# A gated delta rule's solve moved earlier, key norms moved into one block, and a convolution tap moved from VectorE to ScalarE and GpSimd

## The reference

```python
u = rmsnorm(h, norm_mix); proj = u @ w_in                       # 1024 tokens, 1024 -> 2824
aq, ak, av, dq, dk, dv, dz, db, da = split(proj)
qkv = silu(causal_conv(concat(dq, dk, dv), conv_w))             # four taps for each channel
qc, kc = l2norm(q) * 128 ** -0.5, l2norm(k)                     # 4 heads of 128
beta = sigmoid(b); g = -exp(a_log) * softplus(a + dt_bias)
# in chunks of tokens, g a running sum inside a chunk:
L = strict_lower((k * beta) @ k.T * exp(g_i - g_j))
T = (I + L)^-1                                                  # the solve
u = T @ (v * beta);  w = T @ (k * beta * exp(g))
# scan over the chunks: v_new = u - w @ S; o = (q*exp(g)) @ S + a_qk @ v_new; S = S*d + k_d.T @ v_new
```

## Time and profile before

| | us |
|---|---|
| median of three runs | 2007.3 (2006.78 to 2010.78) |
| the profiled execution's own time | 2006.78 |
| its span, first to last instruction | 2005.0 |
| TensorE busy | 1918.5, 96% of the span |
| VectorE busy | 1202.4, 60% |
| ScalarE busy | 794.9, 40% |
| GpSimd busy | 559.6, 28% |
| mean granted TensorE clock | 0.982 of full |

### The profile page before, as it was taken

One profiled execution on the slowest core, in us unless ns is written; L12 is line 12 of the kernel. 1 busy time (PEld: TensorE's weight loads), 2 busy tenths in 40 slices (PEclk: granted clock), 3 DMA queues, 4 the chain that ended last, 5 costly groups with the idle time before them and its releaser, 6 DMA issues.

```text
span 2005.0 us, 24453 instructions
## 1 busy us (share of the span) xinstructions
PE 1918.5 (96%) x9573; PEld 1583.0 (79%) x9573; DVE 1202.4 (60%) x1802; ACT 794.9 (40%) x1409; POOL 559.6 (28%) x561
## 2 busy tenths in 40 slices
PE   8999899989998999999999999999999999799999
PEld 6778788877776888887788887778988897577687
DVE  4577444454489766658768788446435347566641
ACT  5766122254454333333233335434111136455521
POOL 0041014640074656550000023461523124111100
PEclk9999999998999999999999999999999999899999
DMA  5143422211132454449755520113111314311133
GB/s 154 42 146 107 124 78 87 93 53 42 43 116 93 149 173 132 157 157 393 283 178 207 188 64 28 40 51 127 44 31 32 116 43 143 115 32 33 42 91 98
DMA packets 226187, 216.77 MB, mean 108 GB/s; under 512 B 37320, under 2 KB 166600, under 8 KB 225560
## 3 DMA queue, kind: packets, MB, share of 16 engines
q1 hardware_dynamic: 226072, 215.21, 33.3%
HBM read 154.31 MB, written 60.87 MB: 107 GB/s over the span
## 4 chain that ended last, share of the span: by engine, by line
PE 76%; DVE 11%; ACT 5%; POOL 4%; issue 2%; DMA 2%; SPq 0%; DVEq 0%; POOLq 0%; ACTq 0%
PE ps L337 10%; PE ps L338 10%; PE ps L339 10%; PE ps L1769 4%; PE ps L1770 4%; PE ps L1771 4%; PE ps L2148 4%; PE ps L2150 4%; PE ps L2149 4%; PE ps L350 4%; PE ps L3467 3%; PE ps L574 2%; PE ps L1283 1%; PE ps L3368 1%; DVE fm L978 1%
## 5 line engine op out<-in xcount | busy, mean ns | idle before, releaser
L337 PE MATMUL ps<-xh,whi 128*128 128x512 f32 (+2 forms) x1216 | 484.9, 399 | 10.4 <-DVE wlo L323 5.1
L338 PE MATMUL ps<-xl,whi 128*128 128x512 f32 (+2 forms) x1216 | 464.7, 382 | 0.0
L339 PE MATMUL ps<-xh,wlo 128*128 128x512 f32 (+2 forms) x1216 | 463.9, 382 | 0.0
L337 PEld LDWEIGHTS ps<-xh,whi 128*128 128x128 f32 x1216 | 232.0, 191 | 54.2 <-DVE wlo L323 6.1
L339 PEld LDWEIGHTS ps<-xh,wlo 128*128 128x128 f32 x1216 | 231.7, 191 | 41.6
L338 PEld LDWEIGHTS ps<-xl,whi 128*128 128x128 f32 x1216 | 232.2, 191 | 36.6 <-issue 2.6
L1769 PE MATMUL ps<-oph,wsh 128*128 128x512 f32 x448 | 177.5, 396 | 13.1 <-DVE stu L1881 6.6
L2148 PE MATMUL ps<-dnh_b,dnh_a 128*128 128x512 f32 x448 | 175.8, 392 | 7.5 <-DVE dn_b L2174 7.5
L1770 PE MATMUL ps<-opl,wsh 128*128 128x512 f32 x448 | 176.3, 394 | 0.0
L1771 PE MATMUL ps<-oph,wsl 128*128 128x512 f32 x448 | 176.1, 393 | 0.0
L2150 PE MATMUL ps<-dnh_b,dn_a 128*128 128x512 f32 x448 | 175.5, 392 | 0.0
(11 more groups left out here) (495 smaller groups left out, 3469.1 us busy)
## 6 DMA issues: line engine op xcount, KB each, us to landing
dnr_b<-ff_d SPq DMA_DIRECT2D x28, 1024.0 KB, 7.8
dnr_a<-w_down SPq DMA_DIRECT2D x28, 1024.0 KB, 5.5
wraw<-w_in SPq DMA_DIRECT2D x47, 512.0 KB, 3.9
ff_d<-st SPq DMA_DIRECT2D x64, 256.0 KB, 5.1
ff_d<-stt SPq DMA_DIRECT2D x48, 256.0 KB, 5.1
upx<-w_up SPq DMA_DIRECT2D x16, 512.0 KB, 4.3
upy<-w_up SPq DMA_DIRECT2D x16, 512.0 KB, 5.6
xt<-x SPq DMA_DIRECT2D x8, 512.0 KB, 7.7
```

The lines of the kernel that those rows point to most:

```text
L337: pe.matmul(out, h, xh[:, xk, c0:c1_], start=(n == 0), stop=False)
L338: pe.matmul(out, h, xl[:, xk, c0:c1_], start=False, stop=False)
L339: mm = pe.matmul(out, l, xh[:, xk, c0:c1_], start=False, stop=(n == nk - 1))
```

## The change

It has four parts.

1. GpSimd: the key norms of all eight chunks run in one block, behind the turn of k3, with the Dg of chunks 0 and 1 after the first of them. Before, the two Dg ran in panel 4, three norms in the block, and five after the steps of panel 6. Chunk 0's kT and g move from slot 5 to slot 4 of panel 6.
2. The solve's first rows move to panel 10 (rows 1 to 3), ahead of the taps of v1. No rows stand behind the taps any more.
3. For the v panels tap 3 is a product on ScalarE into a new buffer `fm3`, added by GpSimd to what VectorE has after tap 2; silu waits for that add. The solve's temporary `gtmp` makes room for `fm3`.
4. SyncE: the loads of the queries come behind the stores of the inverse (their buffer overlaps the new `gtmp`), and Tw is loaded ahead of Rw for chunk 0.

```diff
-    Gb, gtmp = M("Gb", 32, [32, 32]), M("gtmp", 94, [256])
+    Gb, gtmp = M("Gb", 32, [32, 32]), M("gtmp", 40, [256])
+    fm3 = M("fm3", 92, [T])
-    solve_rows = {(11, 0): range(1, 7), (11, 1): range(7, 10), (11, 2): range(10, 12), (12, 0): range(12, 16), (12, 1): range(16, 19),
-                  (12, 2): range(19, 22), (13, 0): range(22, 32)}
+    solve_rows = {(10, 1): range(1, 4), (11, 0): range(4, 8), (11, 1): range(8, 13), (12, 0): range(13, 18), (12, 1): range(18, 24),
+                  (13, 0): range(24, 32)}
-                out[4 * hf + (n == 0)] += [("kT", n), ("g", n)]
+                out[4 * hf] += [("kT", n), ("g", n)]
+    def last_tap(kind):
+        return 2 if kind == "v" else 3
...
# silu (ScalarE)
+                if kind == "v":
+                    w.wait_ge(*pool_in.at("conv", "v", j))
+                else:
+                    w.wait_ge(*dve_in.at(*(("ev", kind, j, 512) if kind == "dz" else ("conv", kind, j, 3))))
# behind tap 0 (ScalarE)
+                if kind == "v":
+                    if j > 0:
+                        w.wait_ge(*pool_in.at("conv", "v", j - 1))
+                    act.activation(fm3[:], fmc[:, 3:T + 3], ACT.Copy, scale=conv_taps(kind, j)[:, 3:4]).then_inc(*act_in.up("conv3", j))
# VectorE
-                for tap in range(1, 4):
+                for tap in range(1, last_tap(kind) + 1):
-            for row in solve_rows.get((i, 2), ()):
-                solve_dve(dve, w, row)
# GpSimd, behind the turn of k3 (before: key_norm(range(3)), and range(3, NB) and the Dg elsewhere)
+                for b in range(NB):
+                    pool.tensor_tensor(tkh[:, b, :, :], tkh[:, b, :, :], bc(sm["rk"][:, 4 * b:4 * b + 4].unsqueeze(2), [128, 4, 128]), ALU.mult
+                                       ).then_inc(*pool_in.up("normed", kind, b))
+                    if b == 0:
+                        for n in range(2):
+                            delta_pool(pool, w, "diag", n)
+            if kind == "v":
+                w.wait_ge(*act_in.at("conv3", j))
+                w.wait_ge(*dve_in.at("conv", kind, j, 2))
+                pool.tensor_tensor(fms1[i % 2][:], fms1[i % 2][:], fm3[:], ALU.add).then_inc(*pool_in.up("conv", "v", j))
# SyncE
-                queries(0)
-                queries(1)
                 w.wait_ge(*dve_in.at("row", 30))
                 sp.dma_start(inv_d, Gb[:]).then_inc(*st_inverse.up())
                 w.wait_ge(*dve_in.at("inverse turned"))
                 sp.dma_start(invT_d, GT[:]).then_inc(*st_turned.up())
+                queries(0)
+                queries(1)
+                inverse_straight(0)
                 inverse_turned(0)
-                inverse_straight(0)
```

More of the change, by code:

```diff
@@ L882, in silu @@
             if kind in ("k", "q", "v", "dz"):
-                w.wait_ge(*dve_in.at(*(("ev", kind, j, 512) if kind == "dz" else ("conv", kind, j, 3))))
+                if kind == "v":
+                    w.wait_ge(*pool_in.at("conv", "v", j))
+                else:
+                    w.wait_ge(*dve_in.at(*(("ev", kind, j, 512) if kind == "dz" else ("conv", kind, j, 3))))
                 act.activation(fms1[i % 2][:], fms1[i % 2][:], ACT.Silu).then_inc(*act_in.up("silu", kind, j))
@@ L955, in project_dve @@
                 if conv and i > 1 and c0 == 0:
-                    w.wait_ge(*dve_in.at("conv", *in_panels[i - 1], 3))
+                    w.wait_ge(*dve_in.at("conv", *in_panels[i - 1], last_tap(in_panels[i - 1][0])))
+                    if in_panels[i - 1][0] == "v":
+                        w.wait_ge(*act_in.at("conv3", in_panels[i - 1][1]))
                 if kind == "av":
@@ L1027, in query_rope_pool @@
         w.wait_ge(*act_in.at("turned", "aq", 3, 1))
-        w.wait_ge(*dve_in.at("conv", "v", 3, 3))
+        w.wait_ge(*pool_in.at("conv", "v", 3))
+        w.wait_ge(*dve_in.at("conv", "v", 3, 2))
         w.wait_ge(*ld_c1.at())
@@ L1038, in project_pool @@
         pool.memset(fmc[:, 0:3], 0.0).then_inc(*pool_in.up("pad"))
-        def key_norm(blocks):
-            for b in blocks:
-                pool.tensor_tensor(tkh[:, b, :, :], tkh[:, b, :, :], bc(sm["rk"][:, 4 * b:4 * b + 4].unsqueeze(2), [128, 4, 128]), ALU.mult
-                                   ).then_inc(*pool_in.up("normed", "k", b))
         def turned(kind, j):
@@ L1048, in turned @@
                 w.wait_ge(*dve_in.at("norm", kind))
-                key_norm(range(3))
+                for b in range(NB):
[4 more added lines that the diff above has]
+                            delta_pool(pool, w, "diag", n)
             if kind == "dz":
@@ L1061, in project_pool @@
                 turned(*in_panels[i - 1])
-            if i == 4:
-                for n in range(2):
-                    delta_pool(pool, w, "diag", n)
-            if i == PREP0:
-                key_norm(range(3, NB))
+            if kind == "v":
+                w.wait_ge(*act_in.at("conv3", j))
+                w.wait_ge(*dve_in.at("conv", kind, j, 2))
+                pool.tensor_tensor(fms1[i % 2][:], fms1[i % 2][:], fm3[:], ALU.add).then_inc(*pool_in.up("conv", "v", j))
             if i == 1:
```

## The result

The changed kernel took 2026.4 us (median of 4 runs, 2019.5 to 2027.7) where the kernel before took 2007.5 on the same chip (4 runs, 2006.8 to 2010.8). The ratio over all of these runs is 1.0081, 95% interval 1.0059 to 1.0102, or 16.3 us more (11.8 to 20.5); the two medians alone are 18.9 apart. Slower, as forecast, but by more than the range allowed. The three intervals meet between 11.8 and 13.3 us. The profiled execution took 2025.3 us, its span is 2023.5.

The account below looks back on a forecast made before the run. TensorE carries 76% of the last chain; its large stop is 6.1 us idle at UR 0. Sum: 2006.8 + 5.2 (GT later) + 4.5 (additions) + 0.6 (queue) + 0 (clock) = 2017.1 us, range 2010 to 2022.

Parts of the forecast that it names:

- the late chain through g 1: Projection stage: norms ahead of mt 0 end it at 113.1, 7.2 us later; g 1 starts 6.4 later, at 115.8.
- the new wait of VectorE ahead of row 1: Panel 10: VectorE arrives at 176.7 and waits 6.4 us for Gb, until 183.1.
- the collision: V panels: GpSimd's adds hold up two-input VectorE steps for 0.8 of each add, 4.5 us together.
- a slack of 1.3 us: Solve's start: Gb lands at 178.4, row 1 started at 179.70; shifted 4.7 to 183.1, row 1 is 3.4 later.
- the queue: DMA queue from GT to UR 0: Rw issued behind Tw, 0.6 us more; query loads taken at 0.
- shift of the last Gb loads: From panel 8 on: VectorE 4.6 and TensorE 5.0 us late, so Gb's loads move by 4.7.
- work from row 1 to GT: VectorE's solve: one split (1.2) and one evacuation (0.6) come in, 1.8 us more.
- the clock's 2.1 us: TensorE at g 1: a wait of 5 us lowers the clock, charged 2.1 us.
- a gain at UR 0: TensorE at UR 0: last wait only 2.5 us, so the 2.1 us lost to the lower clock fall away.
- a load of this kind lands about 1.3 us after its last issue: Landing of Gb's last blocks, by Rw's example: issued from 175.69 on, 1.47 us, so landed at 178.4.
- a rival of 5.7: Additions in the v panels: the whole add blocks VectorE, losing 5.7 us, kernel at 2018; no separate chance given.
- The rival of more: Clock also drops at the turns of v1 and v3, or norms take 1.29: 2019 to 2022; chance 0.08.

Follow-up runs that it names:

- The three intervals: Changed kernel against the kernel before, measured three times: 16.3 us more (11.8 to 20.5), 11.5 (8.9 to 13.9) and 9.9 (6.6 to 13.3).
- the two later measurements: The changed kernel, unchanged, measured again against the kernel before: ratios 1.0057 and 1.0049, 11.5 and 9.9 us more.
- the whole: The changed kernel with all four parts against the kernel before: ratios 1.0081, 1.0057 and 1.0049 in three measurements.
- the two without taps: Changed kernel with the four taps back on VectorE, measured twice against the kernel before: 12.7 and 10.7 us more.
- the norms alone: The kernel before with only part 1 (key norms in one block, slot 4 for chunk 0): ratio 1.0035, 7.0 us more.
- the two later profiles of before: The kernel before, unchanged, profiled a second and a third time: 2011.8 and 2013.5 us.
- rows alone: The kernel before with only part 2 (solve rows from panel 10, none behind the taps): ratio 1.0033, 6.6 us more.
- later joins: The kernel before with chunk 0's joins two or three slots later on TensorE: 2.6 and 4.0 us less.

## Why the prediction came out as it did

Forecast: GT and UR 0 9.7 and 10.3 us later, 2017.1 us. UR 0 was 14.4 us later (net, mean of three), and the time 10 to 16 us. The direction was right, and so were the late chain through g 1, the new wait of VectorE ahead of row 1 and the collision. The size of the sum was short by 4.1 us at UR 0: 1.4 for key products that it didn't list, 1.1 for a shift taken too small, 1.0 for a slack of 1.3 us that wasn't there, 0.4 for the queue and 0.2 for the additions. The step that failed as a reading is the slack; the largest term is the one put at nothing. Term by term, from the means of three profiles after and two of before:

| term | predicted | measured |
|---|---|---|
| shift of the last Gb loads | 4.7 | 5.8 |
| less the slack of row 1 against their landing | 1.3 | 0.3 |
| row 1 | 3.4 | 5.5 |
| work from row 1 to GT | 1.8 | 1.8 |
| steps beside the additions | 4.5 | 4.7 |
| steps beside the key products | not listed | 1.4 |
| GT to UR 0 | 0.6 | 1.0 |
| UR 0 | 10.3 | 14.4 |

This doesn't account for the first time alone. By the forecast's own start, 2006.8, and 14.4 us the kernel would have taken 2021.2, inside the range. The median of 2026.4 lies 5.2 above that, and the profile puts most of it ahead of all that the change touches: the sum started from 2006.8, the own time of the odd execution whose turn of k1 came 3.9 us earlier than the changed kernel's, and whose clock stayed at its full level behind the turn of k0. On the other chips the kernel before took about 2013. That the two later measurements (11.5 and 9.9) stand near the forecast's 10.3 is luck too: UR 0 was 14.4 and 14.2 late in their profiles, and stretches that the change doesn't touch gave some of it back (5.0 us in the attention stage in the one, 2.0 between UR 0 and the attention in the other).

- *Right: mt 0, ms 0 and g 1.* Ahead of mt 0 stand eleven instructions at 1.0 us and one split. Mt 0 ended at 116.81 (112.9 less the 3.9 of the turn of k1), predicted 113.1. G 1 came at 115.6 on the same count, predicted 115.8. Its idle time, though, was 2.5 us and not 5, since TensorE had lost time ahead of it: 0.9 at kT 0, 1.3 at g 0, and the clock at the lower level behind them (g 0 took 2.07 us, and the granted clock was 0.66 from 105 to 110).
- *Mis-sized: the shift carried from there, 4.7.* The taps of q1 gave back 1.1 us and not 1.8 (4.58 in place of 5.68; one of the three still took 1.94 beside a Dg). And where the clock also fell at g 1 (a stretch at the lower level around 120 in all three profiles of the whole, in one of the two without taps, not with the norms alone), TensorE and not VectorE carried the shift. Counted from the turn of k1, g 2 starts at 55.0 us without this drop and at 56.5 to 56.6 with it, behind the same stop of 2.4 to 2.5 us, and g 7 at 95.9 and at 97.4 to 97.6 (kernel before: 48.8 and 91.4), so the drop is worth 1.5 us. The last Gb loads came 5.8 us late in the whole, and in the two kernels without taps 4.6 without the drop at g 1 and 6.0 with it; the norms alone had 4.0. The prediction charged the clock's 2.1 us once and set them against a gain at UR 0. Such a gain there was in the third profile only (UR 0 took 1.08 us, behind 1.8 idle), and there the clock had fallen at the turn of v3 instead (0.55 from 225 to 230 us). In the other two, UR 0 waited 4.5 us and took 1.9, as before.
- *Failed: "a load of this kind lands about 1.3 us after its last issue", so "at 178.4".* For Rw that is so, after the change too: 236.97 + 1.86 = 238.83, and UR 0 at 240.19, 1.4 us later. It doesn't carry over to Gb, though both are loads of 16 KB each. The blocks of Gb released row 1 2.8 us behind their last issue in the changed kernel and 3.1 us in the two later profiles of before, in which row 1 waits for them (2.6 to 3.3 in all 14 profiles in which it waits). So there was no slack of 1.3 us to take up part of the shift, only the 0.3 between 3.1 and 2.8. Why Gb takes longer than Rw stays open. In the profile that I had, row 1 started right behind the evacuation, at 179.70; it bounded the landing from above, at 179.7 (2.5 us behind the last issue), and I put it 1.3 us below that with no row for it.
- *Right: VectorE waits ahead of row 1*, 8.1 us and not 6.4, and the 1.8 us of work that moves behind it. The saved taps are eaten by those of v1: rows alone has it as 5.7 us with three taps.
- *Right: the collision; its size partly by luck.* Three steps lost 1.54, 1.60 and 1.56 us against the 1.4, 1.7 and 1.4 predicted. The prediction took 0.8 of an addition and set the full lock against it as a rival of 5.7 (its own 2.5 us would give 6.0: three times 2.5, less 0.6, 0.6 and 0.3 of cover). The traces have the full lock: each step is held until the addition's end. The loss came out near the 0.8 since a split ran at the beginning of each addition and held it up in turn (3.19 and 3.45 us, 2.40 when free), with the evacuation behind it, so that the step came late under the lock.
- *Missed: the key products.* I listed what stands ahead of mt 0 in GpSimd's queue, but not what stands behind the additions. 1.4 us, shown by moving them (row 1 to GT 40.3 in place of 41.8).
- *Mis-sized: the queue.* 0.6 was worked out for Tw's issue, and the two query loads were taken at 0. They take 1.39 us of issue, and Rw went out 3.8 us behind GT's store, not 2.8 + 0.6.
- *The rival of more* was nearer than I gave it: the clock did fall behind the turn of v1 (4.37 us idle in the first profile, and the turn then took 1.97 us) in all three, and in the third also behind that of v3. As far as UR 0 still waited behind them (4.6, 4.5 and 1.8 us), these lay under its wait, as the forecast had assumed.

What stays open: why an identical stop is followed by the lower level in one execution and not in another. It is some 5 us in the attention stage and 1.6 behind the turn of k0, and with it and the 5.5 us between profiles behind the up-projection's first load, the differences between 16.3, 11.5 and 9.9 us can't be settled further.

## What to carry over

An instruction that is moved to another engine changes that engine's queue for everything behind it: list what stands behind a new wait as carefully as what stands ahead of it. A wait that the profile doesn't show has no known slack: a consumer that starts right when its data may have landed gives a bound on the landing, not a reserve. And in these runs an operation on GpSimd that reads SBUF cost VectorE up to nearly its whole length (2.07 us of 2.40), even against steps of a third of a microsecond, so put it where VectorE reads PSUM or stands still.

## What was not expected of the hardware

- The same stop of TensorE, 2.7 us at the turn of k0, left the clock at its full level in one of three profiles of the kernel before and not in the other two; 2.4 us in the attention stage the same. Behind a stop of 3.54 us (turn of v3) the next group ran at full level, 1.09 us, and the granted clock stayed 1.00 to 235 us. Behind 3.38 us (UR 0 with later joins) the group also took 1.08 us, but the clock was 0.66 from 225 to 230 us. In the third profile of the changed kernel the turn of v3, behind 3.31 us, took 1.97.
- One small VectorE step waits for all of a GpSimd instruction that reads SBUF: 0.38 us became 2.45 beside an addition of 2.40, and 1.95 beside one of 1.96. Fills of a buffer of that size leave it alone.
- The last four blocks of Gb, 16 KB each, become visible to VectorE 2.6 to 3.3 us after their last issue; four blocks of Rw of the same size to TensorE after 1.4.
